# A hybrid attention and PEER layer pair: attention steps dealt to cycles by tile shape of TensorE

## The chip, the cores and the metric

One core of a Trainium2 chip (trn2) runs the whole program in one launch. The metric is the device time in microseconds, the median of the runs.
## The reference, cut to what matters

Two layers, 1024 tokens, model width 1024. Each layer has three attention branches of 4 heads of 32, gates and an output projection, a layer norm, and a PEER feed-forward: per token 4 x 8 experts are chosen from 16384, and one row of each of two tables is read for each.

```
for l in range(2):
    proj = x @ w_in
    o_sb   = stick_breaking(q, k, v)           # softplus sums over key tiles of 128, last tile first
    o_nsa  = g0*compressed + g1*selected + g2*window(512)   # compressed: 63 keys; selected: 8 blocks of 64
    o_moba = moba(q, k, v)                     # blocks of 256, own block and top 3
    mix = sigmoid(merge_g) * (o @ w_br), summed over the 3 branches
    x = layer_norm(a*x + mix @ w_out)
    # PEER: queries, top 8 of 128 per half, top 8 of 64, 32 rows of u and of v per token
    act = gelu(sum(u[idx] * x));  y = sum(softmax(top) * act * v[idx])
    x = layer_norm(a*x + y)
```

For the selected, window and MoBA branches a softmax over keys needs its own normalizer first: the kernel makes scores by rows (queries on partitions) for maximum and sum, and then once more by keys for the weighted values.

## The kernel before, in words

The 1024 tokens of a layer are two groups of 4 tiles of 128 tokens (GT = 4), so there are 4 groups g = 0 to 3; even groups hold tiles i = 0 to 3 of a layer, odd ones i = 4 to 7. Each group is two sections of 2 tiles for the part behind the attention. A fifth list, g = 4, is the last section's end.

All engines walk one list of steps per group, `STEPS[g]`, made by `steps_of`. It begins with the head (`head_steps`: transposes, projections, the previous group's second section) and goes on with five phases. In phase p run side by side: `gate_steps` (24 gates a group, 4 parts each, 128-row products with a ring of weights), the early section from phase 3 on (`early_section`: merges, outs, queries), `row_steps` of tile p (row scores), and `key_steps` and `stick_steps` of tile p-1. `steps_of` gives each stream's steps positions from 0 to 1 by their weights (the fourth entry) and sorts all of them by position, so that steps of different streams alternate. This order is that of every engine's instructions.

The steps and their lines. A *score* (L1089) is one product of a head's 128 queries with 1 to 4 blocks of 128 keys; window keys lie on partitions 64 to 96, MoBA keys on 0 to 32, selected keys from 64. It goes to bank 0 or 1 in turn (`row_bank`), and waits until VectorE has read the use before the last of the same bank (L1777 adds a mask, takes the minimum and writes the scores to SBUF). ScalarE's exponential (L1389) follows the last chunk of a unit. Tiles 4 to 7 have two chunks per unit, tiles 0 to 3 one. *zc* (L1070) are the compressed scores, *weigh* VectorE's weights for them, *turn_c*, *chosen* and *shift* transposes (L868). *keys* (L1124) makes two score blocks by keys in banks 2 and 3, and on the diagonal a mask product (L1128); a MoBA and a selected block lie in different halves of the partitions, two window blocks in the same. ScalarE exponentiates them (L1406), and *values* (L1139) sums them into bank 7 with 32-column products. *stick* (L1150) are stick-breaking scores in banks 4 and 5, *suffix* (L1158 to L1168) the running sums in the same bank, *sticks* (L1174) the value products. A merge (L886) and a gate (L1056) of the first section use one bank, 6, and wait for its reader: VectorE (L1673) or ScalarE (L1371).

The shape of TensorE's tile is set by a product's rows and columns: 64 for zc, score and keys, 32 for cmp, values and sticks, 128 for the rest.

GpSimd issues one indirect gather of 128 rows of 4 KB per expert step (1024 in all, L840), into 6 slots, later 15. VectorE consumes each (L1520 for table u, L1535 for table v, 1.2 to 1.3 us), except some of the last, which TensorE sums (L1189). `expert_shares` walks the lists with the times of `cost` and says between which steps VectorE does which expert steps: as many, at `EXPERT_US` = 1.33 each, as end at most 3 us after TensorE's planned time. What is left after the last list is the tail. The weights of gates, merges, outs and queries come by SP's queue through a ring of 4 items of 512 KB, each released by TensorE's last use.

## Time and profile before

| what | us |
|---|---|
| median of 3 runs | 2838.77 (2834.23 to 2860.42) |
| span of the profiled execution | 2819.9 |
| the median above that span | 18.9 |
| PE busy | 2453.4 (87%) |
| DVE busy | 1942.6 (69%) |
| POOL busy | 1233.1 (44%) |
| ACT busy | 786.9 (28%) |

The page gives the profiled execution's span alone, without what lies around it. TensorE (PE) is shown in two rows, products (PE) and weight loads (PEld). A product's end is modelled, so neighbouring products overlap in the profile, and the time from one start to the next is the better measure of its cost. The groups' attention stages begin at about 73, 607, 1309 and 1892 us and end at 471, 1172, 1742 and 2457; the fifth list ends at 2553.

### The profile page before, as it was taken

To read this page: it belongs to the slowest core of one execution; us is meant where nothing else is said; L and a number is where in the kernel's file an instruction comes from. 1 tells how busy PE (TensorE), PEld (TensorE's weight loads), DVE (VectorE), ACT (ScalarE), POOL (GpSimd) and SP (SyncE) were. 2 spreads that over 40 slices of the span, in tenths; PEclk is the share of its full clock that TensorE was granted. 3 is DMA by queue.
4 is the path that set the end of the run, shared out by engine and by line. 5 is a ranking of instruction groups with operands and counts; after the bars stand their busy time and mean duration, and the time that the engine had idled before them with its cause. 6 is when DMAs were issued, how large, how long until landed. Compare 5 with 4: busy or idle time off the path is not lost.

```text
span 2819.9 us, 30185 instructions
## 1 busy us (share of the span) xinstructions
PE 2453.4 (87%) x10632; PEld 1484.2 (53%) x10632; DVE 1942.6 (69%) x4009; ACT 786.9 (28%) x1563; POOL 1233.1 (44%) x1028
## 2 busy tenths in 40 slices
PE   8998998998999989899988887999989999987126
PEld 4764476575445357657654465476445347644012
DVE  0122245588988875667886887587998886687875
ACT  2243222213344332321342212212445333301001
POOL 0000023354565432434553655164656352656775
PEclk9998999999989999999997998999999899999569
DMA  4323258787888776977896999787889685998998
GB/s 144 105 73 100 90 188 337 273 290 253 304 283 302 266 251 224 379 286 270 323 359 246 338 375 350 272 297 255 298 297 330 221 308 200 394 366 317 362 373 320
DMA packets 224183, 776.98 MB, mean 276 GB/s; under 512 B 23200, under 2 KB 39712, under 8 KB 219552
## 3 DMA queue, kind: packets, MB, share of 16 engines
q0 software_dynamic: 147456, 536.94, 52.1%
q1 hardware_dynamic: 73696, 227.80, 22.6%
q10 hardware_dynamic: 2880, 10.31, 0.9%
q8 instruction: 85, 1.39, 0.2%
q14 instruction: 66, 0.54, 0.1%
HBM read 766.56 MB, written 8.39 MB: 275 GB/s over the span
## 4 chain that ended last, share of the span: by engine, by line
PE 57%; DVE 15%; DMA 9%; issue 8%; POOL 7%; ACT 3%; another core or an unknown queue 0%; DVEq 0%; ACTq 0%; SPq 0%
PE ps L1056 14%; PE ps L931 7%; PE ps L900 6%; PE ps L984 6%; PE ps L1089 5%; POOL rows L840 4%; DVE x L1535 4%; DMA rows<-in_table_u,idx 4%; PE ps L886 3%; DMA rows<-in_table_v,idx 3%; PE ps L1124 3%; DVE rows L1520 2%; PE ps L1150 2%; DMA wring<-in_merge 2%; PE ps L993 2%
## 5 line engine op out<-in xcount | busy, mean ns | idle before, releaser
L840 POOL DMA_INDIRECT rows<-in_table_u,idx x462 | 565.2, 1223 | 1021.3 <-DVE idx L1643 506.7
L1056 PE MATMUL ps<-xT,wring 128*128 128x256 f32 x3072 | 768.1, 399 | 56.5 <-DMA wring<-in_merge 24.6
L840 POOL DMA_INDIRECT rows<-in_table_v,idx x434 | 526.5, 1213 | 490.5 <-DVE x L1535 362.4
L1056 PEld LDWEIGHTS ps<-xT,wring 128*128 128x128 f32 x3072 | 586.2, 197 | 245.4 <-issue 90.4
L1520 DVE CUSTOM_DVE_ANT_0 rows<-rows,x 128x1024 f32<-128x1024 f32 x462 | 555.0, 1223 | 120.0 <-DMA rows<-in_table_u,idx 114.3
L1535 DVE SCALAR_TENSOR_TENSOR x<-rows,wts,x 128x1024 f32<-128x1024 f32 x413 | 529.8, 1283 | 65.6 <-DMA rows<-in_table_v,idx 43.6
L1089 PE MATMUL ps<-KA,QA 33*128 33x512 f32 (+7 forms) x576 | 253.7, 537 | 26.5 <-DVE part_m L1777 12.9
L1389 ACT ACTIVATE scratch<-scratch,negm 128x640 f32<-128x640 f32 (+7 forms) x192 | 143.5, 747 | 475.3 <-DVE negm L1777 464.6
L900 PE MATMUL ps<-wring,G 128*128 128x512 f32 x384 | 184.8, 617 | 9.7 <-DVE G L1678 6.3
L1777 DVE CUSTOM_DVE_ANT_0 scratch<-ps,cst 128x128 f32<-128x128 f32 (+3 forms) x192 | 86.9, 454 | 143.0 <-PE ps L1089 140.3
L886 PE MATMUL ps<-oT,wring 128*128 128x256 f32 x384 | 126.0, 464 | 53.0 <-DVE G L1673 35.1
L1089 PEld LDWEIGHTS ps<-KA,QA 33*128 33x128 f32 (+1 forms) x576 | 87.9, 193 | 145.6 <-issue 98.9
L1124 PE MATMUL ps<-QA,KA 64*128 64x512 f32 x408 | 157.8, 649 | 1.3 <-ACT scratch L1406 1.3
L1189 PE MATMUL ps<-rows,scratch 128*128 128x512 f32 x84 | 47.1, 694 | 123.3 <-DMA rows<-in_table_v,idx 113.0
L1406 ACT ACTIVATE scratch<-ps 128x1024 f32<-128x1024 f32 (+1 forms) x108 | 104.9, 971 | 146.3 <-PE ps L1124 81.1
L886 PEld LDWEIGHTS ps<-oT,wring 128*128 128x128 f32 x384 | 81.8, 229 | 100.6 <-DVE G L1673 51.6
L900 PEld LDWEIGHTS ps<-wring,G 128*128 128x128 f32 x384 | 69.9, 193 | 107.5 <-issue 91.8
L1371 ACT COPY G<-ps 128x512 f32<-128x512 f32 x96 | 55.9, 582 | 249.2 <-PE ps L1056 233.0
L931 PE MATMUL ps<-G,wring 128*128 128x256 f32 x512 | 117.5, 383 | 4.5 <-ACT G L1285 2.7
L1673 DVE SCALAR_TENSOR_TENSOR G<-G,ps 128x512 f32<-128x512 f32 x96 | 65.1, 686 | 78.9 <-PE ps L886 68.9
L984 PE MATMUL ps<-xT,scratch 128*128 128x512 f32 (+1 forms) x256 | 114.3, 593 | 0.7 <-ACT xT L1304 0.7
L931 PEld LDWEIGHTS ps<-G,wring 128*128 128x128 f32 x512 | 95.7, 190 | 29.3 <-issue 11.3
(209 smaller groups left out, 2951.4 us busy)
## 6 DMA issues: line engine op xcount, KB each, us to landing
wring<-in_merge SPq DMA_DIRECT2D x216, 512.0 KB
wring<-in_w_out_h SPq DMA_DIRECT2D x48, 512.0 KB
wring<-in_w_query SPq DMA_DIRECT2D x32, 512.0 KB
G<-in_w_query SPq DMA_DIRECT2D x12, 1024.0 KB, 8.5
G<-in_x SPq DMA_DIRECT2D x16, 512.0 KB, 4.6
G<-in_ln SPq DMA_DIRECT2D x8, 1024.0 KB, 6.8
G<-x_mid SPq DMA_DIRECT2D x16, 512.0 KB, 5.4
rows<-in_table_u,idx POOLq DMA_INDIRECT x462
```

Of the source, the lines that this page charges most:

```text
L840: pool.indirect_dma_start(row_slot(n), None, tab_u if table == "u" else tab_v, bass.IndirectOffsetOnAxis(ap=idx[:, GT * (g % 2) + t, e:e + ...
L886: mm = pe.matmul(piece(sec, kind, a)[:, SW * n:SW * (n + 1)], w[:, 512 * hf + P * c:512 * hf + P * (c + 1)], oT[:, b, toks], start=True, s ...
L900: mm = pe.matmul(piece(sec, kind, k), turned(0, c, t)[:, 0, :], w[:, 512 * n:512 * (n + 1)], start=(c == 0), stop=(c == KC - 1))
L931: mm = pe.matmul(piece(sec, kind, k)[:, SW * n:SW * (n + 1)], w[:, lo:lo + P], G[:, 1, s_, SW * kc:SW * (kc + 1)], start=(kc == 0 and n == ...
L984: mm = pe.matmul(bank(PROJ_BANK[j])[0:cols.stop - cols.start, :], w[:, c - c0, cols], xT[:, c, :], start=(c == 0), stop=(c == KC - 1))
L1056: mm = pe.matmul(gate_bank(p)[:, SW * n:SW * (n + 1)], w[:, lo:lo + P], xT[:, kc, SW * (p // HALF_GATES):SW * (p // HALF_GATES + 1)], star ...
L1089: pe.matmul(z[:, 0:nb * P], q, k, start=True, stop=True, skip_group_check=True).then_inc(rows_done, 1)
L1124: mm = pe.matmul(bank(2 + n), k, q, start=True, stop=True, skip_group_check=True)
L1389: nc.scalar.activation(z, z, ACT.Exp, scale=-1.0, bias=negm[:, col:col + 1], accum_out=den[:, col:col + 1]).then_inc(probs, 1)
L1406: nc.scalar.activation(PT[N % 2][:, 0:w], pair(2)[:, 0:w], ACT.Exp, scale=-1.0).then_inc(weights_ready, 1)
L1520: v.tensor_tensor_reduce(row, row, x1[:, t, :], 1.0, 0.0, ALU.mult, ALU.add, dots[:, t, e:e + 1]).then_inc(row_used, 1)
L1535: v.scalar_tensor_tensor(out=y, in0=row, scalar=wts[:, t, e:e + 1], in1=y, op0=ALU.mult, op1=ALU.add).then_inc(row_used, 1)
```

## The change

The streams are no longer sorted by position. Each phase is made of cycles: in each first the 64-row products (row scores with a keys step in their middle or behind them), then the 128-row products (gates or the early section, suffix, stick, the transposes, and the mask product of the next cycle's keys), then the 32-column value products. Row scores of a head are listed as window and MoBA of one chunk, then of the next. `full_array` puts the suffix and the late stick product where two neighbouring fill steps share a bank. The mask product becomes a step of its own, ahead of the keys product, which then accumulates on it. zc of a group's first tile follows two pairs; the squeeze uses banks 4 and 5 and no longer 0 and 1. The planner's costs change with it: the second score of a pair costs it next to nothing, a change of shape `CHANGE`, and the factor on TensorE's time in the attention is one constant, `STEADY`.

```
+def row_cycles(t, i):
+    def score(u, c):
+        return ("score", t, (u, c), 0.21 * row_chunks(u, i)[c][1] if u % 2 == 0 or u >= 8 else 0.02)
+    zc = ([("zc", t, 0, 0.5)], [], [])
+    pairs, chosen = [], []
+    for h in range(NH):
+        chunks = range(len(row_chunks(2 * h, i)))
+        pairs.append(([score(u, c) for c in chunks for u in (2 * h, 2 * h + 1)], [], []))
+    slc = [[score(u, c) for c in range(len(row_chunks(u, i)))] for u in range(8, 12)]
+    slc = [(a, [], []) for a in (slc if i >= 4 else [slc[0] + slc[1], slc[2] + slc[3]])]
+    order = pairs[0:2] + [zc] + pairs[2:] if t == 0 else [zc] + pairs
+    at = 2 if t == 0 else 1
+    order[at][1].append(("weigh", t, 0, 0.0))
+    order[at + 1][2].append(("turn_c", t, 0, 0.4))
+    if i >= 4:
+        order[4][2].append(("chosen", t, 0, 0.2))
+    return order + slc + [([], [("log_sum", t, 0, 0.0)], [("shift", t, 0, 0.2)])]
+def stick_cycles(t, i):
+    def stick(m):
+        return [("stick", t, m, 0.86)] if m <= i else []
+    out = [([("spread", t, 0, 0.0)] + stick(0) + stick(1), [("soft", t, 0, 0.0)], [])]
     for m in range(i + 1):
-        steps.append(("suffix", t, m, 1.8))
-        if m + 2 <= i:
-            steps.append(("stick", t, m + 2, 0.9))
-        if m >= 1:
-            steps.append(("sticks", t, m - 1, 0.9))
-    return steps + [("sticks", t, i, 0.9)]
+        out.append(([("suffix", t, m, 1.72 if m else 1.1)], stick(m + 2), [("sticks", t, m, 0.25)]))
+    return out
...
+def shared_bank(before, step):
+    if before is None or step[0] != before[0]:
+        return False
+    return step[0] == "merge" or step[0] in ("gate", "out", "query") and step[2][0] != before[2][0]
+def full_array(fill, early, late):
+    gaps = [x for x in range(1, len(fill)) if shared_bank(fill[x - 1], fill[x])]
+    x = gaps[0] if gaps else min(1, len(fill))
+    y = gaps[-1] if len(gaps) > 1 else len(fill)
+    return fill[:x] + early + fill[x:y] + late + fill[y:]
+def phase_steps(g, phase, fill):
+    half = g % 2
+    i, t = GT * half + phase - 1, phase - 1
+    rows = row_cycles(phase, i + 1) if phase < GT else []
+    jobs = key_jobs(i) if phase > 0 else []
+    first = 1 if i == 0 else 0
+    count = max(len(rows), len(jobs) + first)
+    narrow = [[] for _ in range(count)]
+    keys = {first + p * (count - first) // len(jobs): p for p in range(len(jobs))}
+    sticks = {}
+    if phase > 0:
+        groups = stick_cycles(t, i)
+        at = sorted(keys)
+        sticks = {at[r * len(at) // len(groups)]: groups[r] for r in range(len(groups))}
+    whole, done, out = sum(st[3] for st in fill), 0.0, []
+    fills = [[] for _ in range(count)]
+    for st in fill:
+        fills[min(count - 1, int(count * done / whole))].append(st)
+        done += st[3]
+    for c in range(count):
+        score, later, ends = rows[c] if c < len(rows) else ([], [], [])
+        key, values = [], []
+        if c in keys:
+            p = keys[c]
+            halves, masked = key_parts(i, p)
+            key, values = [("keys", t, p, 0.86 * halves)], [("values", t, p, 0.43)]
+            if p == 0:
+                values = [("cmp", t, 0, 0.3)] + values
+        if c + 1 in keys and masked_jobs(i, keys[c + 1]):
+            ends = ends + [("mask", t, keys[c + 1], 0.22 * len(masked_jobs(i, keys[c + 1])))]
+        parts = len(score) // 2 if i >= 3 else 0
+        out += (score[:parts] + key + score[parts:] if parts or len(score) != 1 else score + key) + later
+        early, late, weighted = sticks.get(c, ([], [], []))
+        fill = full_array(fills[c], early, late)
+        at = 1 if later and later[0][0] == "log_sum" else len(fill)
+        out += fill[:at] + ends + fill[at:] + values + weighted
+    return out
...
     for phase in range(GT + 1):
-        streams = []
         if phase < 3:
-            streams.append((0.0, sum([gate_steps(p) for p in range(share[phase], share[phase + 1])], []), 1.0))
+            fill = sum([gate_steps(p) for p in range(share[phase], share[phase + 1])], [])
         else:
-            streams.append((0.0, early_section()[phase - 3], 0.95))
+            fill = early_section()[phase - 3]
+        if phase == 0:
+            fill = [("squeeze", 0, 0, 3.0)] + fill
+        out += phase_steps(g, phase, fill)
         if phase > 0:
-            i = GT * half + phase - 1
-            streams += [(0.0, key_steps(phase - 1, i), 1.0), (0.0, stick_steps(phase - 1, i), 1.0)]
-        if phase == 0:
-            streams += [(0.1, [("squeeze", 0, 0, 3.0)], 0.1), (.35, row_steps(phase, GT * half + phase), .65)]
-        elif phase < GT:
-            streams.append((0.0, row_steps(phase, GT * half + phase), 0.85))
-        placed = []
-        for n, (begin, steps, span) in enumerate(streams):
-            whole, at = sum(st[3] for st in steps), 0.0
-            for k, st in enumerate(steps):
-                placed.append((begin + span * at / whole, n, k, st))
-                at += st[3]
-        out += [st for _, _, _, st in sorted(placed, key=lambda a: a[:3])]
-        if phase > 0:
-            out.append(("done", phase - 1, 0, 0.5))
+            out.append(("done", phase - 1, 0, 0.3))
     return out
...
+SHAPES = {"zc": 64, "score": 64, "keys": 64, "cmp": 32, "values": 32, "sticks": 32}
...
-            now += (.78 if kind in HEAD_KINDS or s < 0 else 1.12 if not late else 1.0 if g % 2 else 1.1) * pe
+            now += (.78 if kind in HEAD_KINDS or s < 0 else STEADY) * pe
+            if pe > 0.0 and SHAPES.get(kind, 128) != shape:
+                shape, now = SHAPES.get(kind, 128), now + CHANGE
...
+STEADY, CHANGE = 1.02, 0.2
...
+                        if t == 0 and a == (0, 0):
+                            pe.wait_ge(proj_copied, 6 * g + 4)
+                            pe.wait_ge(v_copied, 2 * (g + 1))
+                            pe.wait_ge(zeros_set, 2 + 2 * GT)
+                            pe.wait_ge(const_landed, 16)
...
+                        masked = [n for n, _ in masked_jobs(i, a)]
                         for n, (branch, b) in enumerate(jobs):
                             keys_ = slice(P * b, P * (b + 1))
                             if branch == "moba":
                                 k, q = KA[0:64, 0, keys_], QA[0:64, t, :]
                             else:
                                 k, q = KA[64:128, branch == "win", keys_], QA[64:128, t, :]
-                            mm = pe.matmul(bank(2 + n), k, q, start=True, stop=True, skip_group_check=True)
-                        for n, (branch, b) in enumerate(jobs):
-                            if b == i or (branch == "win" and b == i - 4):
-                                mask = M_KEEP if b == i else M_EDGE
-                                mm = pe.matmul(bank(2 + n).rearrange("p (h q) -> p h q", h=NH), masks[:, M_ID:M_ID + P],
-                                               masks[:, mask:mask + P].unsqueeze(1).to_broadcast([P, NH, P]),
-                                               start=False, stop=True, skip_group_check=True)
+                            mm = pe.matmul(bank(2 + n), k, q, start=n not in masked, stop=True, skip_group_check=True)
                         mm.then_inc(keys_done, 1)
+                    elif kind == "mask":
+                        N = pairs_before(T) + a
+                        if N >= 1:
+                            pe.wait_ge(weights_ready, N)
+                        for n, own in masked_jobs(i, a):
+                            mask = M_KEEP if own else M_EDGE
+                            pe.matmul(bank(2 + n).rearrange("p (h q) -> p h q", h=NH), masks[:, M_ID:M_ID + P],
+                                      masks[:, mask:mask + P].unsqueeze(1).to_broadcast([P, NH, P]),
+                                      start=True, stop=False, skip_group_check=True)
```

## Rows read from the trace of the kernel before

**Rows 1.** Windows of the stages: start:end, length, busy us (count) per engine, TensorE's granted clock, DMA share, GB/s

```profile
73.00:471.00 398.00, 370.68 (x1750) 239.99 (x1749) 126.92 (x387) 114.97 (x263) 41.53 (x36) 0.97 0.43 148
607.00:1172.00 565.00, 523.62 (x2497) 304.59 (x2495) 450.13 (x927) 193.58 (x361) 271.76 (x221) 0.94 0.79 280
1309.00:1742.00 433.00, 381.01 (x1748) 244.99 (x1746) 344.86 (x656) 115.28 (x273) 230.18 (x189) 0.94 0.87 322
1892.00:2457.00 565.00, 523.36 (x2498) 304.98 (x2496) 462.33 (x950) 192.71 (x360) 283.54 (x230) 0.94 0.80 285
2457.00:2553.00 96.00, 78.69 (x277) 53.12 (x278) 67.19 (x108) 14.83 (x21) 53.76 (x45) 0.91 0.97 373
2553.00:2820.00 267.00, 117.70 (x238) 44.74 (x236) 205.45 (x354) 24.31 (x71) 184.74 (x169) 0.75 0.90 341
```

**Rows 2.** Groups by line: busy us, mean ns, idle before

```profile
L1089 PE MATMUL ps<-KA,QA 33*128 33x512 f32 (+7 forms) x576 | 253.7, 537 | 26.5 <-DVE part_m L1777 12.9 <-DVE negm L1777 9.3 <-DVE negm_c L1748 2.4
L1124 PEld LDWEIGHTS ps<-QA,KA 64*128 64x128 f32 x408 | 49.3, 191 | 55.0 <-issue 47.6 <-DVE negm L1777 5.9
L1520 DVE CUSTOM_DVE_ANT_0 rows<-rows,x 128x1024 f32<-128x1024 f32 x462 | 555.0, 1223 | 120.0 <-DMA rows<-in_table_u,idx 114.3 <-issue 1.1 <-DVE gw L1660 0.2
```

**Rows 3.** Timeline of TensorE, 721 to 731 us: start, length, what

```profile
721.60 1.13 PE L1124 MATMUL ps<-QA,KA 64*128 64x512 f32 x4
722.65 1.12 PE L1162 MATMUL ps<-scratch,cst 128*128 128x512 f32 x2
723.62 1.02 PE L1168 MATMUL ps<-scratch,cst 128*128 128x512 f32 x2
724.48 0.60 PE L868 MATMUL ps<-cst,cand 128*47 128x128 f32 x4
...
727.56 0.64 PE L1139 MATMUL ps<-scratch,vals 128*32 128x128 f32 x16
728.13 1.12 PE L1089 MATMUL ps<-KA,QA 33*128 33x512 f32 x2
729.18 1.13 PE L1150 MATMUL ps<-q_heads,k_sb 128*128 128x512 f32 x2
730.24 0.49 PE L1089 MATMUL ps<-KA,QA 33*128 33x128 f32 x2
```

**Rows 4.** Timeline of TensorE, 756 to 774 us

```profile
756.95 1.88 PE L1124 MATMUL ps<-QA,KA 64*128 64x512 f32 x4
758.67 1.02 PE L1089 MATMUL ps<-KA,QA 49*128 49x512 f32 x2
...
772.77 0.65 PE L1139 MATMUL ps<-scratch,vals 128*32 128x128 f32 x16
773.23 0.40 PE L1174 MATMUL ps<-scratch,vals 128*32 128x128 f32 x8
```

**Rows 5.** Waits of TensorE: us in total, times, longest us

```profile
PE ps L886 <- DVE G L1673: 35.1, 23, 5.4
PE ps L1056 <- ACT G L1371: 19.6, 22, 4.0
PE ps L1089 <- DVE part_m L1777: 12.9, 8, 2.5
```

**Rows 6.** Timeline of VectorE, 745 to 749 us

```profile
745.45 0.41 DVE L1777 CUSTOM_DVE_ANT_0 scratch<-ps,cst 128x256 f32<-128x256 f32 x1
745.79 2.67 DVE L1535 SCALAR_TENSOR_TENSOR x<-rows,wts,x 128x1024 f32<-128x1024 f32 x2
748.38 0.74 DVE L1777 CUSTOM_DVE_ANT_0 scratch<-ps,cst,part_m 128x512 f32<-128x512 f32 x1
```

**Rows 7.** Window of an odd group's phases 0 to 3

```profile
607.00:1021.00 414.00, 378.29 (x1701) 203.07 (x1700) 358.63 (x714) 148.94 (x287) 216.57 (x175) 0.93 0.80 280
```

57 lines of the change are left out of this document (19 added, 38 removed).

## The prediction

> **What bounds the kernel now.** I read the windows by stage first. In the attention stages, the four stretches of [rows 1] with TensorE over 87% busy (398, 565, 433 and 565 us, together 1961 of the span's 2820), TensorE is the engine that is nearly always busy: 371 of 398, 524 of 565, 381 of 433, 523 of 565. VectorE comes second (450 of 565, or 80%), and the DMA engines third, at 0.79 to 0.87. After 2457 us TensorE has nothing left but the last section, and at 2553 the tail begins: 267 us in which the gathers (DMA share 0.90) and VectorE (205 us) finish the expert rows. So time taken from TensorE's list in the attention stages comes off the end, as long as VectorE and the gathers can keep up, and what they can't keep up with is added to the tail.
>
> Then the timeline of TensorE says what its busy time is made of. A busy TensorE isn't one at its rate, so I go by starts. Two passes of 512 columns take 0.86 us when the next product has the same shape (L1168, 723.62 to 724.48) [rows 3]. The same two passes take 1.05 us as a row score of 33 rows followed by a 128-row product (L1089, 728.13 to 729.18), and 1.06 us as a 128-row product followed by a score (L1150, 729.18 to 730.24). Sixteen value passes take 0.57 us before a score [rows 3] and 0.46 us before other value passes [rows 4]. A change of tile shape thus costs 0.1 to 0.2 us, on each side. And four passes of 512 columns with 64 rows, two in the lower and two in the upper half of the array, take 1.05 us (L1124, 721.60 to 722.65) [rows 3], as much as the two passes of one score: halves of the array work at the same time. Four in one half take 1.72 us (756.95 to 758.67) [rows 4].
>
> **The change, part by part.**
>
> 1. *Changes of shape.* Written out from the step lists of the kernel, an even group's attention has 159 changes between the shapes 128, 64 and 32, an odd group's 265: 848 in all. From the new rules I count by cycles. A cycle is one block of 64-row steps, one of 128 and, where it has values or sticks, one of 32. An even group has 8, 8, 8, 8 and 6 cycles, the last of the first four without scores: 14 + 16 + 17 + 19 + 18 = 84. An odd group has 10, 10, 10, 10 and 11: 18 + 26 + 27 + 30 + 33 = 134. That is 436, so 412 go. The price: into 64 rows about 0.1 (1.06 for 0.86 is the dear case, other 128-row steps show half of it), out of 64 rows 0.19, out of 32 rows 0.11; one trip 128, 64, 32, 128 costs about 0.4 for three changes. I take 0.14 each: **-58 us**. Bounds: 0.09 and 0.2 each, -37 and -82.
>
> 2. *Row scores as pairs.* A window score and a MoBA score of the same head sit in different halves (rows 64 to 96, and 0 to 32) and go to banks 1 and 0. Before, another stream's step nearly always stands between them, and each pays its full 0.43 us per pass of 512 columns. In pairs the shorter one is hidden, 0.213 us per block of 128 keys. Tiles 0 to 3: 4 heads x (1+2+3+4) blocks x 0.213 = 8.5 us per even group. Tiles 4 to 7: the first chunks share 1 block, the second 4, so 4 heads x 4 tiles x 5 x 0.213 = 17 us per odd group. Together **-51 us**; L1089 has 253.7 us now [rows 2]. Bounds: 0 if they don't overlap, -51. I take all of it, since the key products show the very overlap.
>
> 3. *Full-array products at the bank gaps.* Consecutive gates or merges share a bank and wait for its reader: 35.1 us on VectorE's merges and 19.6 us on ScalarE's gate copies, 45 waits [rows 5]. The new lists put a suffix or stick product into at most two such gaps per cycle, but they also put merges next to each other that had a score between them. I take **-20 us** of the 54.7, bounds +20 and -54.
>
> 4. *New waits at the second half of a pair.* For tiles 4 to 7 a head has four scores on two banks. The third needs VectorE's read of the first, the fourth that of the second. Only a keys step (0.86 us) lies between. The reads are 0.41 + 0.08 and up to 0.74 + 0.08 us, and one or two expert steps (2.67 us for two) often stand between VectorE's reads [rows 6]. Behind a waiting score stand all of TensorE's later steps, and behind those ScalarE's exponentials and gate copies. There are 16 such places in an odd group, 32 in all; half of them meeting one expert step of 1.28 us, less 0.4 of cover, is 14 us: **+15**. Bounds: 0 and 32 x 2.5 = +80, with the longest such wait seen now, 2.5 us [rows 5].
>
> 5. *Masks ahead, squeeze in banks 4 and 5, zc after two pairs, constants' waits moved.* The 56 mask products stay as many; they only move out of the keys step into the 128-row block (their saving is in term 1). There they wait for the exponential of the keys pair before, with the second scores and the gates of the cycle between; that cover gone, a mask waits some 1 us. The squeeze no longer holds the row banks, and two pairs now cover ScalarE's copy of it. Nothing is counted; uncovered, it would be some 3 us a group. SP issues the same loads in the same order, released by the same steps.
>
> 6. *Expert steps and the tail.* The planner deals expert steps by TensorE's planned time at a fixed 1.33 us each, so a shorter plan gives fewer steps before the tail, though the shorter time between routings pulls the other way. I expect 0 to 14 of 1024 to slide, and take 7. In the tail 169 gathers were issued in 267 us, 1.58 us each [rows 1]: **+11 us**, bounds 0 and +22.
>
> 7. *Clock.* The granted clock is 0.94 in the attention stages after the first [rows 1]: 6% of about 1560 us, 94 us, plus 12 of the first. The half-clock stretches follow TensorE's waits. With fewer waits at banks and new ones at pairs I take 0; bounds -50 and +50.
>
> Sum: -58 - 51 - 20 + 15 + 11 = -103 us on the profiled span of 2819.9, so 2717. The median of the runs is 18.9 us above that span, so **2735 us** in the median (-3.7%).
>
> One row speaks on weight loads. Four passes in one half of the array run at 0.43 us each, 1.72 in all [rows 4], though each has a load of 191 ns [rows 2]; the loads stay hidden behind products in the same rows. The Trainium skill (TensorE: Matmul & The Clock Gate, Part 3: Packing small matmuls) says loads overlap running products only when their row group differs. By that rule each of the 108 keys steps, now set directly behind or between scores of the same halves, would expose one load, and the sum would end some 20 us higher. The trace does not agree with it here, so I leave it out.
>
> **The rivals.**
>
> *VectorE becomes the bound.* For it: from 607 to 1021 us VectorE is busy 359 of 414 us, 87% [rows 7]. Steps 1 and 2 want about 34 us of that stretch and 380 us would be 94%. Against it: the planner can move expert steps to the next stretch, where VectorE is at 91 of 151. If VectorE can't go above 90% there, the stretch ends at 398 and not 380, 18 us lost, twice 36, and some 12 more steps slide into the tail, 19 us: about 2790. In the third group the gathers are at 0.87 and 322 GB/s; at the 373 GB/s of the stretch after 2457 [rows 1] it could shrink to 374 us, so they don't bind first.
>
> *The pairs don't overlap.* This is the change not doing what it says: VectorE's lag makes the second score of a pair start after the first. Then the 51 us stay, and 2786 is the time. Against it stands only that keys pairs do it; for it, that the banks of a second-chunk pair come free one read (0.82 us) apart.
>
> *Slower: reads behind expert steps.* At the 32 places of term 4, TensorE waits not for one expert step but for several. Each place must cost 4.1 us more before the 103 us and 1% more (28) are gone, which is three expert steps of 1.28 and the read. Four of them make 5.1 us, 163 us, and with the lower clock that follows waits 2890. Against it: the reads' waits now come to 12.9 us over 8, the longest 2.5 [rows 5]; for it, that steps of other streams lay between nearly all scores before, and afterwards one keys step.
>
> *More than forecast.* If both bank waits and half of the lost clock go as well, 34 and 50 us, it is 2650.
>
> **How the numbers follow.** Forecast 0.52, VectorE bound 0.16, no overlap 0.11, slower 0.11, more 0.10. The forecast's own range is 2690 to 2780. About 1% is what a measurement of this kernel can tell from no change, so the lines are 2810 and 2867. Of the forecast's 0.52 about 0.03 lies above 2810, of each rival near 2790 a quarter, and of the slower one 0.02 below 2867: faster 0.79, the same 0.12, slower 0.09. The range reaches down by the clock's bound and up to both rivals near 2790: 2675 to 2805.
>
> **What would show it.** Right: per head, window and MoBA score start within a few ns of each other; an odd group's attention takes about 530 us where it took 565, an even group's about 410 of 433, the first 375 of 398; two 512-column passes of a score are followed after 0.86 to 1.05 us by the next shape half as often; L1056's waits for ScalarE's copy shrink. The tail stays near 267 us plus 11. Wrong: waits of L1089 for L1777 well over 60 us in sum (term 4), VectorE above 92% from the second group on with TensorE idle, a granted clock under 0.92 in the attention stages, or a tail over 290 us.

## The result and the profile after

The changed kernel takes **2875.21 us** in the median of 15 runs (2851.94 to 2891.08), the kernel before 2845.05 in 15. The ratio is 1.010, with a 95% interval of 1.0080 to 1.0121: slower, by about what was held to be the least that can be told from no change. The forecast was 2735 (2675 to 2805), a gain of 3.7%. The profiled execution has a span of 2874.1 us, 54.2 more than before.

The page's first part, engine by engine (busy us, share of the span, instructions):

```profile
span 2874.1 us, 30221 instructions
PE 2367.9 (82%) x10640; PEld 1500.0 (52%) x10640; DVE 1943.1 (68%) x4007; ACT 787.0 (27%) x1565; POOL 1242.7 (43%) x1028
```

TensorE has lost 85 us of busy time and the span has grown. VectorE, ScalarE and GpSimd are as busy as before (1943, 787 and 1243 us against 1943, 787 and 1233). So the gain on TensorE is there, and more than the whole of it has come back as idle time. The windows of the same stages, whose bounds have moved (they answer to [rows 1]):

```profile
73.00:452.00 379.00, 347.76 (x1744) 241.09 (x1744) 125.66 (x388) 112.93 (x262) 40.41 (x36) 0.98 0.45 154
587.00:1161.00 574.00, 493.59 (x2498) 309.80 (x2497) 454.19 (x946) 194.32 (x362) 270.60 (x223) 0.93 0.78 276
1316.00:1735.00 419.00, 361.64 (x1749) 247.24 (x1748) 321.22 (x615) 113.77 (x270) 215.72 (x175) 0.95 0.86 314
1908.00:2466.00 558.00, 494.70 (x2496) 310.77 (x2495) 450.67 (x909) 194.11 (x361) 271.79 (x220) 0.93 0.78 278
2466.00:2575.00 109.00, 80.83 (x280) 54.19 (x280) 71.10 (x124) 14.55 (x21) 60.33 (x49) 0.87 0.92 346
2575.00:2874.00 299.00, 127.59 (x240) 47.00 (x240) 215.76 (x367) 24.94 (x73) 204.45 (x179) 0.74 0.87 324
```

The four attentions take 379, 574, 419 and 558 us against 398, 565, 433 and 565: 31 us less. The heads between them take 135, 155 and 172 against 136, 137 and 150, the fifth list 109 against 96, the tail 299 against 267. TensorE's waits (engine and line, waited for: us, times, longest), of the changed kernel:

```profile
PE ps L950 <- DMA wring<-in_merge: 44.2, 3, 41.9
PE ps L950 <- DVE G L1745: 41.9, 25, 10.5
PE ps L1156 <- DVE part_m L1849: 38.8, 17, 8.8
PE ps L1222 <- ACT q_heads L1482: 28.4, 13, 4.5
PE ps L1230 <- DVE scratch L1797: 24.1, 3, 10.2
PE ps L1120 <- ACT G L1443: 9.2, 9, 2.5
```

Against [rows 5]: the gates' wait for ScalarE's copy is halved (19.6 to 9.2). The merges' wait for VectorE is not (35.1 to 41.9). The scores' wait for VectorE's read of the chunk before tripled (12.9 to 38.8). Here part_m is what VectorE writes when it has read the first chunk of a unit from its bank. Three are far longer than before: the stick products' wait for ScalarE's copies into q_heads (28.4 us, 1.4 before), the first suffix's for VectorE (24.1, 2.1 before), and one merge stands for 41.9 us, for its weights (14.0 before).

The pairs overlap, but the second pairs only in part. This is TensorE's timeline of one cycle of an odd group in the changed kernel:

```profile
906.34 0.70 PE L1156 MATMUL ps<-KA,QA 33*128 33x128 f32 x3
906.66 0.59 PE L1192 MATMUL ps<-QA,KA 64*128 64x512 f32 x1
906.88 0.59 PE L1156 MATMUL ps<-KA,QA 33*128 33x512 f32 x1
907.10 1.23 PE L1192 MATMUL ps<-QA,KA 64*128 64x512 f32 x3
907.94 1.73 PE L1156 MATMUL ps<-KA,QA 33*128 33x512 f32 x4
909.60 1.13 PE L950 MATMUL ps<-oT,wring 128*128 128x256 f32 x4
```

The eight score passes and the four passes of the keys step take 3.26 us from first start to next shape. The last four, the second pair of the head, take 1.66 of it (907.94 to 909.60). Among 128-row products, as the run e5_second sets them, the same four passes take 1.06, no more than the 1.05 of one score alone [rows 3]:

```profile
770.95 1.13 PE L1161 MATMUL ps<-KA,QA 33*128 33x512 f32 x4
772.01 1.12 PE L1227 MATMUL ps<-q_heads,k_sb 128*128 128x512 f32 x2
```

Of the 32 second pairs of the odd groups, 19 take 1.06 us there. In the changed kernel none does: at full clock 21 take 1.17 to 1.79 us and two 2.4 to 2.5, and the nine that the half clock touched take 1.8 to 2.5. In sum they are 24 us over 1.06 each, beside the waits in front of them. In twelve of them the second score starts only when VectorE has read that score's bank, 0.57 to 1.36 us behind the first score's start; for the others the trace names no such wait.

Since a product's end is modelled, I added up the whole of TensorE's time by starts: each step lasts to the next step's start, and is split into its products at full clock (the shortest such step of its kind with the same shape behind it), up to 0.2 us at a change of shape, half of the time at the half clock, and the rest, waits. For the profiled executions, in us:

```
                       attention: products  changes  half clock  waits | heads and fifth list | tail | span
kernel before                     1473      144      89          256   |  589                 | 266  | 2820
changed kernel                    1420       48      90          375   |  641                 | 299  | 2874
difference                         -53      -96      +1         +119   |  +52                 | +33  |  +54
```

The first 3 us or so of a span, before TensorE's first product, are in none of the columns. How the -149 us divides between products and changes hangs on the rule of the split. If a step's shortest duration is taken apart by which score or keys step stands next to it, products lose 78 and changes 71, and the waits grow by 115. The sum of the first two and the waits stay, and the single rows of the next table move too (second pair, odd: 7 before and 41 after).

The same split by what stands behind a wait, in us (excess over the products, in the attentions; "second pair" is the chunk-1 scores of tiles 4 to 7):

```
                              before  changed  e4_spread  e5_second  e13_mid  e15_first
second pair, odd                12      65       66         28         31       10
first pair, odd                 23      13       13         31         32       24
first pair, even                 3      13       14         14         14        7
stick, all phases                5      40       16         37          7        6
first suffixes, last phase       4      34       38         31         33        6
gates, all                      84      58       67         56         59       79
merges, phases 0 to 3           28      32       34         29         33       32
```

### The profile page after: what moved, and what is told of

The parts are those of the page before. It is cut to its first block, busy times and chain, and to the rows that moved or that the text cites. A ratio compares the mean times of both kernels' runs of the same rounds, so it can differ in the third digit from the quotient of the medians.

```text
span 2874.1 us, 30221 instructions
## 1 busy us (share of the span) xinstructions
PE 2367.9 (82%) x10640; PEld 1500.0 (52%) x10640; DVE 1943.1 (68%) x4007; ACT 787.0 (27%) x1565; POOL 1242.7 (43%) x1028
## 4 chain that ended last, share of the span: by engine, by line
PE 42%; DVE 19%; DMA 14%; POOL 11%; issue 10%; ACT 3%; DVEq 0%; another core or an unknown queue 0%; ACTq 0%; SPq 0%; POOLq 0%
PE ps L1120 11%; POOL rows L904 8%; DMA rows<-in_table_v,idx 6%; PE ps L964 6%; DVE x L1607 6%; PE ps L1156 4%; DMA rows<-in_table_u,idx 4%; PE ps L1048 4%; PE ps L995 3%; PE ps L950 3%; DMA wring<-in_merge 2%; PE ps L1192 2%; DVE rows L1592 2%; PE ps L1222 1%; POOL xT L904 1%
## 5 line engine op out<-in xcount | busy, mean ns | idle before, releaser
L904 POOL DMA_INDIRECT rows<-in_table_u,idx x454 | 556.2, 1225 | 1059.6 <-DVE dots L1592 538.2
L1120 PE MATMUL ps<-xT,wring 128*128 128x256 f32 x3072 | 747.3, 398 | 33.7 <-DMA wring<-in_merge 17.6
L1120 PEld LDWEIGHTS ps<-xT,wring 128*128 128x128 f32 x3072 | 593.1, 198 | 227.8 <-issue 97.0
L1592 DVE CUSTOM_DVE_ANT_0 rows<-rows,x 128x1024 f32<-128x1024 f32 x454 | 545.9, 1223 | 110.2 <-DMA rows<-in_table_u,idx 105.9
L1156 PE MATMUL ps<-KA,QA 33*128 33x128 f32 (+7 forms) x576 | 196.3, 529 | 47.0 <-DVE part_m L1849 38.8
L950 PE MATMUL ps<-oT,wring 128*128 128x256 f32 x384 | 113.8, 427 | 90.2 <-DMA wring<-in_merge 44.2
L950 PEld LDWEIGHTS ps<-oT,wring 128*128 128x128 f32 x384 | 74.6, 209 | 137.7 <-issue 69.6
L1156 PEld LDWEIGHTS ps<-KA,QA 33*128 33x128 f32 (+1 forms) x576 | 75.9, 192 | 115.6 <-DVE part_m L1849 56.4
L1222 PE MATMUL ps<-q_heads,k_sb 128*128 128x512 f32 x144 | 82.5, 675 | 34.6 <-ACT q_heads L1482 28.4
## 6 DMA issues: line engine op xcount, KB each, us to landing
G<-in_w_query SPq DMA_DIRECT2D x12, 1024.0 KB, 10.4
```

What stands on the lines that cost most here:

```text
L904: pool.indirect_dma_start(row_slot(n), None, tab_u if table == "u" else tab_v, bass.IndirectOffsetOnAxis(ap=idx[:, GT * (g % 2) + t, e:e + ...
L950: mm = pe.matmul(piece(sec, kind, a)[:, SW * n:SW * (n + 1)], w[:, 512 * hf + P * c:512 * hf + P * (c + 1)], oT[:, b, toks], start=True, s ...
L1120: mm = pe.matmul(gate_bank(p)[:, SW * n:SW * (n + 1)], w[:, lo:lo + P], xT[:, kc, SW * (p // HALF_GATES):SW * (p // HALF_GATES + 1)], star ...
L1156: pe.matmul(z[:, 0:nb * P], q, k, start=True, stop=True, skip_group_check=True).then_inc(rows_done, 1)
L1222: pe.matmul(bank(4 + M % 2), k_sb[:, P * (i - a):P * (i - a + 1)], q_heads[:, T % 2, :, :].rearrange("p h n -> p (h n)"), start=True, stop ...
L1592: v.tensor_tensor_reduce(row, row, x1[:, t, :], 1.0, 0.0, ALU.mult, ALU.add, dots[:, t, e:e + 1]).then_inc(row_used, 1)
```

## The experiments

All ratios are against the kernel before on the same chip; the changed kernel's own is 1.010 (1.0080 to 1.0121). The experiments ran on several chips, and the changed kernel was not timed again beside them, so a difference of some tenths of a per cent between an experiment and the changed kernel is not sure. Stage lengths and waits are those of one profiled execution each. Where an expectation is in us, I turn it into a ratio with the 2845 us of the kernel before.

**The pace of the deal (e1_pace).**

```
-STEADY, CHANGE = 1.02, 0.2
+STEADY, CHANGE = 1.2, 0.2
```

> The changed kernel with STEADY 1.2 in place of 1.02, nothing else. The order of TensorE's steps is the same; the planner's TensorE is slower, so it deals 49 expert steps and not 80 to an odd group's last phase, 39 and not 55 to the head of the fourth group, and 167 and not 146 to an odd group's phases 0 to 3. Theory A (the deal: the gain of the phases 0 to 3 is lost because expert steps slid into the last phase, the heads and the tail): the odd groups' last phase falls from 174 and 163 us to about 150, the fourth group's head from 172 to 150, and the whole lies at 2790 to 2820, below the kernel before. Theory B (the chains: TensorE waits inside each cycle for VectorE's reads, and an expert step in front of a read is paid in full): 21 more expert steps in phases 0 to 3 cost up to 1.3 us each, the phases go from 400 to about 425 us, what the last phase gives back is used up, and the whole stays within 1% of 2875.

Measured: 1.0045 (1.0015 to 1.0074), between the two. The odd phases 0 to 3, in the changed kernel (first line) and here (second):

```profile
587.00:987.00 400.00, 345.04 (x1701) 204.52 (x1701) 319.10 (x693) 149.08 (x285) 177.48 (x146) 0.93 0.73 252
```

```profile
584.00:1004.00 420.00, 352.93 (x1700) 207.56 (x1699) 359.68 (x701) 148.71 (x286) 221.91 (x178) 0.91 0.80 280
```

With the expert load of the kernel before (359 us of VectorE in 414 us, [rows 7]) the new order needs 420, and in the fourth group 429 against 415. The last phase gave back 14 and 5 us, the fourth head 32, the tail 37. The deal explains about half of the loss, and no gain is hidden behind it. What the phases 0 to 3 gained in the changed kernel, 14 and 19 us, they gained with 30 expert steps less each.

**VectorE's expert steps made thin (e2_thin_after, e2_thin_before) and halved (e10_half_after, e10_half_before).**

```
-v.tensor_tensor_reduce(row, row, x1[:, t, :], ...        # and the like for table v
+v.tensor_tensor_reduce(row[:, 0:64], row[:, 0:64], x1[:, t, 0:64], ...     # halved: 0:512
```

> The changed kernel with VectorE's expert steps on 64 of 1024 columns (L1592, L1607; most of their arithmetic is left out), all gathers, the order and the deal of the steps unchanged. To be read against the same edit of the kernel before, in the attention stages alone. Theory B with expert steps as the cause: TensorE's waits in the attention fall from some 375 us to under 200 and the stages lose about the 119 us by which they grew. If the waits are ScalarE's and VectorE's own work in the cycle, without expert steps, they stay above 250. If the gathers or weights are late, they stay too, and TensorE's waits name DMA.

> The kernel before with the same edit: VectorE's expert steps on 64 of 1024 columns. With expert steps as the cause of the new waits, the changed kernel's attention stages are shorter than these by the 150 us that products and changes of shape gave (by the starts on TensorE); with the cycle's own chains as the cause, by less than 80.

> The changed kernel with expert steps on 512 of 1024 columns on VectorE (half of their arithmetic is left out), some 0.75 us a step. If VectorE's load is what holds the phases 0 to 3, the odd groups' length lies near that with thin steps, 361 to 370 us, since a busy share of 60% is then no limit, and not half way (380) between 361 and 400.

> The kernel before with the same edit. Thin steps gave 402 us for the odd phases 0 to 3, full ones 414: by either theory 402 to 408 us here. The difference between the two kernels should be 35 to 40 us in these phases.

These kernels leave out most (thin) or half of the expert arithmetic, and there is one execution of each. With thin steps the attentions take 1845 us in the new order and 1939 in the old; with half steps 1829 and 1866; with full ones 1932 and 1962. The new order's waits are 325, 314 and 375, so most of the new ones stay when VectorE's load is small. The wait that term 4 of the prediction is about doesn't: the scores' wait for part_m falls from 38.8 us to 15.4 with half steps and to 8.6 with thin ones (9 waits):

```profile
PE ps L1156 <- DVE part_m L1849: 8.6, 9, 2.7
```

The odd groups' phases 0 to 3 take 361 and 362 us in the new order with thin steps, 372 and 369 with half, 400 and 396 with full ones. So half the load gives back nearly all that thin steps do, as expected if VectorE's load holds them (361 to 370) and not half way (380). For the kernel before the expectation failed: 374 and 382 us came, and not 402 to 408. Half steps were expected to leave 35 to 40 us between the kernels in these phases, and left 2 in the second group and 13 in the fourth. Windows of the changed kernel and of the kernel before, both with half steps:

```profile
586.00:958.00 372.00, 335.91 (x1701) 200.50 (x1699) 237.00 (x648) 149.56 (x286) 147.57 (x144) 0.96 0.75 267
```

```profile
609.00:983.00 374.00, 354.60 (x1700) 191.68 (x1699) 259.88 (x683) 148.92 (x288) 181.14 (x173) 0.99 0.85 307
```

The thin run of the kernel before took longer there (402 us) than its half run (374), at a granted clock of 0.93 against 0.99. By the split the half clock explains most of that in the second group (in the attention 32 us lost to it against 5) and little in the fourth (24 against 19). So the thin pair's 94 us, which lies between what either theory had asked (150, or under 80), is not to be read as a price of expert steps.

**Pairs (e3_pairs).** The kernel before, with window and MoBA scores of a head next to each other, all streams still sorted by position. It also moves the step chosen from behind the seventh score unit to behind the eighth, directly in front of the first selected score, which waits for it:

```
+        if u < 8 and u % 2 == 1:
+            for c in range(len(row_chunks(u, i))):
+                steps.append(("score", t, (u - 1, c), 0.0))
+                steps.append(("score", t, (u, c), <weight of both>))
```

> The kernel before with one part of the change alone: window and MoBA scores of a head and chunk next to each other, the streams still dealt by position, the deal of expert steps as before (840 ahead of the tail). If a pair's overlap is worth its products, 51 us, and the waits behind it are few: 2785 to 2805. If the second pair of a head waits for VectorE's reads of the first as in the changed kernel (tiles 4 to 7, 32 places), the odd groups gain nothing and it lies at 2825 to 2850, with waits of the scores for part_m over 40 us.

Measured: 1.0031 (0.9995 to 1.0067), no gain. The products fell by 40 us and the changes by 37, and the waits grew by 84, in the attentions (by the other rule of the split 45 together, and 49). The odd groups' attentions took 571 and 580 us against 565. Its waits:

```profile
PE ps L1094 <- DVE part_m L1782: 24.3, 7, 6.0
PE ps L1094 <- DVE QA L1604: 21.7, 8, 5.3
```

The rival came out in time, though 24.3 us for part_m is under the 40 expected. The 21.7 us for QA all stand at the first selected score of a tile, eight times: they are the price of the moved step chosen and not of the pairs. Both are the pattern of the whole: two steps put together save their time, and the step of another stream that stood between them no longer covers what the second waits for.

**Two places (e4_spread, e5_second).**

```
 e4:  +    if phase > 0:
      +        out.append(("spread", t, 0, 0.0))      # at the phase's start, not in front of stick 0
 e5:  -        out += score[:parts] + key + score[parts:] ...
      +        out += score[:parts] + key + later     # tiles 4 to 7
      +        fill = fill[:half] + score[parts:] + fill[half:]
```

> The changed kernel with the step spread (ScalarE's four copies into q_heads) at the start of its phase and no longer directly in front of the first two stick products. Theory: in the changed kernel a stick product stands right behind what feeds it, and TensorE waits 28 us for the copies (L1222 on q_heads, 13 times) and 12 us more; the waits have nothing to do with expert steps. Then L1222's wait for q_heads falls below 5 us and the whole lies 20 to 30 us below the changed kernel, 2845 to 2855. Rival: the wait is ScalarE's backlog (exponentials of the pairs), stands there either way and moves to the next ScalarE product; the whole stays within 10 us of 2875.

> The changed kernel with one thing moved: for tiles 4 to 7 the second-chunk pair of a head stands in the middle of the cycle's 128-row products and no longer behind the keys step. It costs up to 64 more changes of shape, some 10 us. Theory of the second pair (32 places; scores of chunk 1 stand at 65 us of excess in the odd groups, 12 in the kernel before): the excess falls to under 25 us, the odd groups' phases 0 to 3 from 400 to about 380 us, the whole to 2830 to 2850. Rival (VectorE is simply late by its expert steps, and the wait goes to whatever needs it next): scores improve, but merges, first pairs and gates take the wait over; within 15 us of 2875.

Measured: e4 1.0051 (1.0021 to 1.0081), e5 1.0040 (1.0009 to 1.0071), both below the changed kernel's 1.010, by 14 and 17 us. The wait for q_heads fell from 28.4 us to 4.0 (first line, e4). The second pair's excess fell from 65 to 28, and the wait for part_m from 38.8 to 5.1 (e5), but first pairs took over 18 of the 37. So e4's wait went as its theory said, and the whole gained less than the 20 to 30 us expected. e5 lies with its rival: the odd phases 0 to 3 took 392 us, not 380, and the time waited moved on to the first pairs, which wait for ScalarE's row_buf (15.0 us).

```profile
PE ps L1224 <- ACT q_heads L1484: 4.0, 4, 1.2
```

```profile
PE ps L1161 <- ACT row_buf L1473: 15.0, 9, 2.8
PE ps L1161 <- DVE part_m L1854: 5.1, 2, 2.8
```

**Both places, slower paces (e6_both, e7_both_slow).** STEADY 1.12 and 1.2.

> Both moves together, and STEADY 1.12: 69 expert steps in the fourth group's last phase and not 80, 39 and not 55 in its head. If the waits named add up (second pair -30, copies -25, deal -20): 2795 to 2815, faster than the kernel before. If waits only change places: 2840 to 2860.

> As the one before with STEADY 1.2: 46 expert steps in each odd group's last phase, 170 to 184 in the phases 0 to 3. The first pace run gave 2853 with the old places of the steps. With places mended, 2790 to 2815 if phases 0 to 3 can now hide their expert steps; 2830 to 2850 if they can't.

Measured: 1.0002 (0.9974 to 1.0031) and 1.0108 (1.0050 to 1.0165). By the first the waits only changed places; the second is slower than either of its ranges. With 184 expert steps in the odd phases 0 to 3 these took 435 and 433 us, with 170 they took 419 and 429, with 147 (e5) 392 both times. From one to the next that is 0.3 to 1.6 us for each step more.

**No expert step in front of a read (e8_behind, e9_mended).**

```
-            while nxt < ready:
+            while nxt < ready and kind not in ("zc", "score", "keys"):
```

> The changed kernel, with the planner dealing no expert step behind a 64-row step (zc, score, keys), so that none stands between the reads of a head's first and second pair; 141 of them in an odd group's phases 0 to 3 and not 146. Theory of the read behind an expert step: the second pair's excess (65 us in the odd groups) falls to about the 31 us of the run with thin expert steps, and the whole by 20 to 35 us against the changed kernel, to a ratio of 0.998 to 1.003 against the kernel before. Theory of VectorE's load (TensorE and VectorE share a length that 359 us of VectorE's work fill in 414 to 420 us in either order): the expert steps gather behind the cycle, the waits go to first pairs and suffixes, and the ratio stays at 1.006 to 1.012.

> The same with spread at the start of its phase and STEADY 1.12 (136 to 164 steps in the odd phases 0 to 3). By the theory of places 0.985 to 0.995; by the theory of VectorE's load 0.998 to 1.005, like the earlier run with both moves and STEADY 1.12 (1.0002).

Measured: e8 1.0190 (1.0127 to 1.0253), above the changed kernel's ratio and outside both ranges; e9 1.0012 (0.9988 to 1.0037), in the range of the load theory. The second pair's excess is 60 us, where it was 65, and the wait is there as before:

```profile
PE ps L1156 <- DVE part_m L1849: 34.2, 15, 5.3
```

This doesn't clear the expert steps, because the edit hardly moved them. By the lists, the changed kernel already had only 4 expert steps between the reads of a first and a second pair at all 32 places; e8 has none. They stand ahead of the first pair's read, for which the third score waits, and there they stay. Of the 38.8 us of these waits in the changed kernel VectorE spent 13.4 in expert steps, of the 34.2 in e8 16.4. One of them in e8, TensorE and then VectorE:

```profile
2005.44 0.70 PE L1156 MATMUL ps<-KA,QA 33*128 33x128 f32 x4
2009.55 2.41 PE L1156 MATMUL ps<-KA,QA 33*128 33x512 f32 x4 [3.40 <-DVE part_m L1849]
2006.61 2.67 DVE L1607 SCALAR_TENSOR_TENSOR x<-rows,wts,x 128x1024 f32<-128x1024 f32 x2
2009.20 0.28 DVE L1849 CUSTOM_DVE_ANT_0 scratch<-ps,cst 128x128 f32<-128x128 f32 x1
```

**The forced steps (e11_cliff).** At the fourth group's tanh the planner must have dealt step 531. The kernel before is at 536 by then, the changed one at 515, so 16 come at once.

```
-else STEADY) * pe
+else 1.15 if g == 2 else STEADY) * pe
```

> The changed kernel with the planner's TensorE slower in the third group's attention alone (1.15 in place of 1.02): 39 and not 55 expert steps in the fourth group's head, 18 more before it, 4 fewer in the tail. The order of TensorE's steps is the same. Theory of the forced steps: at the fourth group's tanh the planner must have dealt step 531; the changed kernel is at 515 there and deals 16 at once, and TensorE stands 41.9 us before the first merge. Then that wait is under 10 us, the head falls from 172 to about 148 us, and the ratio from 1.010 to 1.001 to 1.005. Rival: the wait is for the merge weights behind the gathers and has nothing to do with the burst; it stays above 30 us and the ratio within 0.003 of 1.010.

Measured: 1.0042 (1.0021 to 1.0062), as the theory of the forced steps had it. The head fell from 172 to 144 us, and the longest wait of a merge for its weights from 41.9 to 12.1 (under 10 was expected). TensorE's timeline in the changed kernel, and the merges' wait in this run:

```profile
1735.53 1.06 PE L932 MATMUL ps<-cst,G 128*128 128x128 f32 x8 [0.69 <-ACT G L1443]
1778.52 2.04 PE L950 MATMUL ps<-oT,wring 128*128 128x256 f32 x4 [41.92 <-DMA wring<-in_merge]
```

```profile
PE ps L950 <- DMA wring<-in_merge: 18.5, 4, 12.1
```

Of the 28 us, 13 came back in the third group's attention (432 against 419), which now has the steps. How 16 forced steps keep a merge's weights away isn't shown. It isn't VectorE's arithmetic alone: with the same deal the longest such wait is still 37.4 us with half expert steps and 28.8 with thin ones.

**The repairs together (e12_places, e13_mid).** e11 with both places; e13 with STEADY 1.06 besides.

> The same with spread at the start of the phase and the second-chunk pair inside the 128-row products. If the three repairs add (ratios 1.0051 and 1.004 of the single ones against 1.010, and the forced steps): 0.990 to 0.997. If places only move waits: 1.000 to 1.005.

> As e12 with STEADY 1.06: 156 expert steps in an odd group's phases 0 to 3 (147 and 170 were tried), 842 ahead of the tail. The run with STEADY 1.12 gave 1.0002. By the prices read so far (0.65 to 1.1 us for a step in the odd phases 0 to 3, 2 us in the tail) the middle is no worse than either: 0.990 to 1.000.

Measured: 0.9894 (0.9858 to 0.9930) and 0.9872 (0.9839 to 0.9904), both faster than the kernel before; e12 lies at the edge of its range (0.990 to 0.997) and e13 a little below its own (0.990 to 1.000). The attentions of e13 take 370, 567, 423 and 564 us. Against 398, 565, 433 and 565 the gain is that of the first group (28) and some of the third (11); the odd groups have none.

**Where it pays (e14_even, e15_first).** The new cycles in the even groups alone, and in the first group alone; elsewhere the streams, costs and factors of the kernel before (its mask product still a step of its own, directly ahead of its keys). In e14 the planner's factor in the third group is 1.18.

```
     half = g % 2
+    if half:            # e15: if g > 0:
+        <streams sorted by position, as before>
+        return out
```

> The new cycles in the even groups alone (spread at the start of the phase), the kernel before's streams and deal in the odd groups (steps per phase 27, 46, 45, 58, as there). Theory: where VectorE has room the cycles pay, where it hasn't they don't. The first group has no expert steps and the third few in its phases 0 to 3; with spread moved the two even attentions took about 366 and 406 to 420 us against 398 and 433. So the ratio is 0.980 to 0.988, faster than both kernels. If it is the total of VectorE's and the gathers' work after the first group that sets the end, only the first group's 32 us come through or less: 0.988 to 0.997.

> The new cycles in the first group alone (spread at the start of the phase), all else in the order and with the deal of the kernel before. The first group's attention has no expert steps before its last phase. If what the cycles gain comes through only where VectorE has room, this run has nearly all of it: the first attention 366 to 371 us against 398, nothing else changed, ratio 0.988 to 0.992. If the third group's 11 us and the odd groups' places carry a good part of the 1.3% of the last two kernels, it is 0.993 to 0.997.

Measured: 0.9870 (0.9842 to 0.9899) and 0.9867 (0.9825 to 0.9908). e14 lies in its range, but not by its theory: the third group gave nothing. e15 lies a little below its own. The first group alone has the whole of the gain that any version reached. Its attention in e15, and the second group's:

```profile
75.00:443.00 368.00, 341.67 (x1748) 237.96 (x1746) 123.59 (x384) 112.93 (x262) 39.96 (x34) 1.00 0.46 158
581.00:1138.00 557.00, 514.99 (x2498) 299.30 (x2496) 450.76 (x914) 193.25 (x362) 277.95 (x223) 0.96 0.80 285
```

By starts the first attention takes 369 us against 398; the third group's in the kernel e14 took 439, none gained. Some 10 of the 29 us are the clock's: TensorE's granted clock there is 1.00 where it was 0.97 [rows 1], and by the split the half clock cost 2 us and not 12. That is no accident of one execution. In the first group's attention it cost 12 to 14 us in each of the four profiles of the old order (the thin, half and e3 kernels included) and 2 to 9 in each of the sixteen of the new one.

**Mended places at half load (e16_half_mid).** e13 with half expert steps.

> The kernel of e13_mid with VectorE's expert steps on 512 of 1024 columns (half of their arithmetic is left out). At half load the kernel before took 521 and 537 us for the odd groups' attention and the changed kernel 528 and 522: no gain there either. If what eats the odd groups' gain is the places (second pairs and spread behind their sources), then with the places mended the odd attentions at half load fall to 490 to 505 us. If the waits of the new order are spread over all its steps (merges, shifts, first pairs, sticks), they stay at 510 to 530.

Measured, in one execution: 537 and 536 us, over both ranges. The places that were moved are mended (second pair 25 us, stick 6), and waits at first pairs, first suffixes, keys and shifts stand in their stead. Against the changed kernel at half load (528 and 522) the clock hides what they may have given. These are the odd attentions here (first two lines) and there:

```profile
588.00:1124.00 536.00, 484.33 (x2494) 301.88 (x2492) 329.66 (x901) 192.43 (x361) 227.91 (x221) 0.95 0.81 293
1833.00:2369.00 536.00, 486.33 (x2496) 302.09 (x2496) 335.58 (x913) 193.40 (x362) 236.58 (x230) 0.95 0.81 298
586.00:1114.00 528.00, 480.63 (x2497) 303.87 (x2494) 330.80 (x899) 194.45 (x362) 223.22 (x221) 0.96 0.81 296
1824.00:2346.00 522.00, 476.97 (x2498) 301.48 (x2498) 331.87 (x896) 197.05 (x362) 225.65 (x221) 0.97 0.81 298
```

By the split the half clock took 26 and 30 us here and 19 and 14 there, which is the whole difference of 23 us.

## Why the prediction was wrong

**The terms on TensorE held, and gave more.** Terms 1 and 2 forecast -109 us, and the starts give -149: products -53 (pairs, forecast -51), changes of shape -96 (forecast -58). That each term came so near its forecast is the first rule's doing; by the other it is -78 and -71. By the first a change cost 0.17 us before and 0.11 now, not one price for both; part of what stood at a change before was a short wait. The lists hold 848 changes before and 442 after, so 406 went and not 412.

**Term 3 came out by the split and not by the waits that it was priced from.** Gates lost 26 us of excess, merges gained 4: -22 against -20. But the 54.7 us of waits that the term counted are still 51.1: 10.4 less at the gates for ScalarE, 6.8 more at the merges for VectorE. The rest of the gates' gain is of other waits, such as that for their weights, so the near hit is in part luck. The clock (term 7) came out at 0.

**The step that failed is term 4.** It priced what is lost when steps are put together from one place, the second pair, and from one cause, one expert step in front of VectorE's read: +15. At that place the count was right and the price was not. 17 of the 32 places waited, where it took half, but for 38.8 us in all, 2.3 each and not 0.9. The excess there grew by 53 us, waits and slower pairs together.

The cause that it named is one of three. The expert work bears much of the wait, which is 8.6 us with thin steps and 38.8 with full ones; e8 can't speak against it, since it left the steps in front of the first pair's read. The longest waits are of another kind. In both odd groups the second pair of the first head stands 8.8 and 3.9 us behind the routing, VectorE's last work of the head. Row scores used to begin at 0.35 of phase 0 and now begin with it, which the prediction didn't count:

```profile
595.28 0.18 DVE L1715 TENSOR_SCALAR idx<-idxf 128x32 int32<-128x32 f32 x1
595.69 0.29 DVE L1849 CUSTOM_DVE_ANT_0 scratch<-ps,cst 128x128 f32<-128x128 f32 x1
596.04 1.43 PE L1156 MATMUL ps<-KA,QA 33*128 33x512 f32 x2 [8.80 <-DVE part_m L1849]
```

And the third head's second pair of the same tile waits 4.7 and 4.3 us behind the step weigh and two expert steps.

The greater part stands outside the term. The prediction looked for new waits only where a bank was read twice in a cycle. It passed over the stick product behind spread (35 us more, of ScalarE; e4 took 24 back), the first suffixes of the last phase (30), and first pairs in even groups (10). Each was covered before by the other streams' steps, which the sorting by position had put between a source and its user. In place of +15 less 20, TensorE's waits in the attention grew by 119 us, and the prediction had no price for that rule of the list before, that no stream's steps stand together. e3 shows the same on a small scale: the whole of what products and changes gave came back as waits, though 21.7 us of that is the moved step chosen.

**Term 5 counted nothing and was to name its cover.** The squeeze and the masks are indeed not seen in the waits. Spread was not in its list at all. It is a step that the change moved directly in front of its user.

**Term 6 had the sign and not the size.** Ten steps slid into the tail, not 7, and the tail grew by 33 us, 3.3 a step and not 1.58; at e1, 18 steps fewer gave 37 us, 2.1 each. The forced steps at the fourth head were in the code and were not read: +22 us in the head, of which e11 took back all and kept 15. The rest of the 52 us in heads and fifth list is 18 in the third head (155 us, where e1, e8 and e11, with the same order of TensorE's steps, took 140 to 147, and e13 159), and 13 in the fifth list.

**The rivals.** That VectorE becomes the bound fits the full load (414 us before, 420 in e1, at 359 and 360 us of VectorE), and in the new order the odd phases 0 to 3 fall by 28 us when its load is halved. But it isn't shown to be the whole cause: at half the load VectorE is at 64%, and the odd groups' attention is hardly shorter than the old order's (528 and 522 us against 521 and 537). The slower rival had the right sign and the right place, and 53 us there, not the 163 that it took to be needed, since it was not alone. That the pairs don't overlap is refuted for first pairs and true in part for second ones, for which it gave the reason itself, that their banks come free one read apart.

**The signs.** The scores of a pair were to start within a few ns of each other; no pair did (0.21 us apart at the least), and e5's pairs of 1.06 us show that it isn't needed. Of the signs of being wrong the tail came (299 us), and the other three did not: the scores' waits for VectorE stayed under 60 us, VectorE at 80% in the odd phases 0 to 3, the granted clock in the attentions at 0.93 or more. The waits that mattered were at other lines.

**What stays open.** Why the odd groups gain next to nothing is not settled. At full and half load it isn't the two places alone (e13, e16, the latter blurred by the clock). The share of the expert steps is open: e8 didn't move them, and the single executions lean towards a share. Against the old order the two odd attentions are 2 us longer in sum with full steps, 8 shorter with half and 60 shorter with thin ones; without what the half clock took, 10, 17 and 41 shorter. The first suffix's wait for VectorE falls with the load as well (24.1 us, 5.7 with half steps). Against the expert steps as the only cause stands, above all, the stick products' wait for q_heads, which doesn't fall (28.4, 36.7 with half steps, 34.2 with thin ones). Which dependences of the cycle hold it was not tried one by one. In the first group the waits rose far less, and it has no expert steps before its last phase; the third group has shorter rows as well and little gain.

## What to carry to other kernels

A list sorted so that streams alternate hides latencies that no row of its profile shows, since nothing waits there. Before steps are put together by shape or bank, write down for each what it waits for and which foreign steps lie between, and price the loss of each, not of the most visible one. And try such an order stage by stage: here one group of four carried the whole gain, 1.3%, and the edit in all groups, with spread still in front of its user, lost 1.0%. When an experiment is to clear a cause, count first how much of it the edit moves: e8 moved 4 expert steps at 32 places. Where a planner has a hard due count, see whether the new pace still meets it.

## What the runs showed of the hardware

A change of tile shape costs TensorE between 0.1 and 0.2 us by the starts of its products [rows 3], and leaving out 406 of them in the attention was worth 71 to 96 us in all, by the rule of the split. Two scores in different halves of the array, four passes of 512 columns, take 1.06 us when both banks are free (e5), as long as one score alone (1.05), and 1.17 to 1.79 us in 21 of the changed kernel's 32 second pairs, at full clock. The granted clock in the later attentions did not rise with fewer changes: 0.93 to 0.95, as before (0.94). In the first one it did, from 0.97 to 0.98 and to 1.00 in e15. After a stand of TensorE it was often the lower of its two levels: the nine second pairs that had waited 1.6 to 8.8 us ran at 1.2 GHz in whole or in part and took 1.8 to 2.5 us, and the 23 that had waited under 0.6 us ran at 2.4 GHz. The clock (third number from the end) behind the wait of 4.7 us, and in the cycle shown above:

```profile
624.00:626.20 2.20, 2.20 (x5) 0.70 (x5) 0.25 (x3) 0.00 (x0) 0.90 (x1) 0.50 0.79 244
906.30:909.60 3.30, 3.30 (x17) 1.48 (x13) 2.66 (x7) 1.02 (x1) 0.48 (x1) 1.00 0.97 328
```
